# Output projections of a two-layer block on one Trainium2 core: five pairs of weight tiles as seven half-width block products

## The reference

```python
y = act @ w_out                          # 512x2048 by 2048x2048, the output projection
x = _layernorm(DEEPNORM_ALPHA * x + y, post_ln_g[i], post_ln_b[i])
x = x + (p[i] @ ple_w[i]) * jax.nn.sigmoid(x @ ple_gate_w[i])
```

## Time and profile before

| | before |
|---|---|
| median of 3 runs | 2104.14 us (2104.05 to 2104.16) |
| profiled execution, span from first to last instruction | 2101.9 us |
| what the median has around that span | 2.2 us |
| TensorE busy, of the span | 2095.9 us (100%) |
| VectorE | 1256.4 us (60%) |
| ScalarE | 818.5 us (39%) |
| GpSimd | 360.7 us (17%) |
| stretch 865 to 887 us (two tiles, layer 0): VectorE, ScalarE, GpSimd busy | 7.16, 3.83, 0 us |
| stretch 930 to 952 us (two tiles with centring): VectorE, ScalarE, GpSimd busy | 16.95, 6.75, 0 us |

### The profile page before, as it was taken

How to read it: one execution, slowest core, us unless ns; L and a number is a source line. 1 busy time by engine, 2 the same in 40 slices (tenths; PEclk the granted TensorE clock), 3 DMA queues, 4 the chain that set the end, 5 groups by cost and what they waited for, 6 DMA issues and landing times.

```text
span 2101.9 us, 28710 instructions
## 1 busy us (share of the span) xinstructions
PE 2095.9 (100%) x10510; PEld 1739.0 (83%) x10510; DVE 1256.4 (60%) x2106; ACT 818.5 (39%) x1042; POOL 360.7 (17%) x193
## 2 busy tenths in 40 slices
PE   9999999999999999999999999999999999999999
PEld 7888888888888888888788888888888888887888
DVE  5225575665755747356733588887888973567332
ACT  4224464563654657123722322222323451227221
POOL 0000000000000004000400034444757520004000
PEclk9999999999999999999999999999999999999999
DMA  8222222122122123322233322222222242222431
GB/s 318 81 100 80 81 81 80 63 77 80 62 98 80 60 80 117 136 97 100 86 124 125 135 89 92 100 100 100 94 88 99 100 179 101 88 94 79 139 112 69
DMA packets 33027, 213.62 MB, mean 102 GB/s; under 512 B 3904, under 2 KB 4176, under 8 KB 9408
## 3 DMA queue, kind: packets, MB, share of 16 engines
q1 hardware_dynamic: 28224, 189.54, 25.6%
q0 software_dynamic: 4448, 22.72, 2.8%
...
## 4 chain that ended last, share of the span: by engine, by line
PE 99%; ACT 1%; DVE 0%; issue 0%
PE G L493 91%; PE X L493 5%; PE T L493 1%; PE T L675 1%; PE T L796 0%; ACT a_hi L907 0%; ACT Z L1099 0%; ACT Y L1171 0%; PE T L801 0%; PE T L647 0%; ACT L991 0%; DVE tmp L1444 0%; PE T L671 0%; DVE Y L1446 0%; DVE tmp L1439 0%
## 5 line engine op out<-in xcount | busy, mean ns | idle before, releaser
L493 PE MATMUL G<-a_hi,w_hi 128*128 128x512 f32 (+1 forms) x2780 | 1084.5, 390 | 0.6 <-ACT a_hi L907 0.6
L493 PE MATMUL G<-a_lo,w_hi 128*128 128x512 f32 (+1 forms) x2780 | 1076.8, 388 | 0.0
L493 PE MATMUL G<-a_hi,w_lo 128*128 128x512 f32 x2764 | 1072.9, 388 | 0.0
L903 ACT ACTIVATE w_hi<-w_raw 128x2048 fp32r<-128x2048 f32 x174 | 333.4, 1916 | 957.5 <-PE G L493 944.1
L1299 DVE TENSOR_TENSOR w_lo<-w_raw,w_hi 128x2048 fp32r<-128x2048 f32 x128 | 297.1, 2321 | 643.0 <-ACT w_hi L903 643.0
L493 PEld LDWEIGHTS G<-a_hi,w_hi 128*128 128x128 f32 x2780 | 521.9, 188 | 110.5 <-ACT a_hi L907 1.5
L493 PEld LDWEIGHTS G<-a_lo,w_hi 128*128 128x128 f32 x2780 | 522.0, 188 | 107.3 <-issue 0.5
L493 PEld LDWEIGHTS G<-a_hi,w_lo 128*128 128x128 f32 x2764 | 518.9, 188 | 107.0 <-issue 0.2
L1888 DVE SCALAR_TENSOR_TENSOR T<-tmp,par,T 128x512 f32<-128x512 f32 x464 | 306.9, 748 | 0.0
L437 POOL TENSOR_TENSOR w_lo<-w_raw,w_hi 128x2048 fp32r<-128x2048 f32 x45 | 207.9, 4620 | 232.2 <-ACT w_hi L903 232.2
L405 POOL TENSOR_TENSOR a_lo<-Y,a_hi 128x512 fp32r<-128x512 f32 x32 | 44.3, 1402 | 366.7 <-ACT a_hi L907 366.4
...
## 6 DMA issues: line engine op xcount, KB each, us to landing
w_raw<-wall_in SPq DMA_DIRECT2D x174, 1024.0 KB, 4.8
...
Y<-xT_in POOLq DMA_DIRECT2D x4, 1024.0 KB, 8.2
...
Y<-x_residual POOLq DMA_DIRECT2D x4, 1024.0 KB, 5.2
...
Z<-xT_in SPq DMA_DIRECT2D x6, 512.0 KB, 9.4
```

Of the source, the lines that this page charges most:

```text
L493: return pe.matmul(o, l, r, start=start, stop=stop)
L903: f(w_hi[:, w.slot, :], w_raw[:, w.slot, :], ACT.Copy).then_inc(S("w_hi"), 1)
```

## The change

The first four tiles of the output projection are done as before (two as a pair, two by `gemm`). Tiles 4 to 13 become five pairs (`p` = 2 to 6). In each pair the first 4 of the 16 input chunks are done plainly for both tiles (pieces `r1`, `r2`: 12 matmuls of 512 columns each). The other 12 chunks are seen as two groups of 6, the two tiles as two columns and the tokens as two halves of 256; of this 2x2 by 2x2 block product seven products are formed in place of eight, each 6 blocks x 3 matmuls of 256 columns. Four of them use weights as loaded (`b11`, `b22`, `b21`, and the plain token halves) or sums of them (`t1`, `t3`, `t2`, `t4`, made by GpSimd); three kinds of combined activations are made once per layer (`fold_operands` on GpSimd, copied by ScalarE, split by VectorE: `folds`). VectorE combines the products as it takes them from PSUM (`empty_first`, `empty_products`, `finish_two`, `finish_one`). Tiles 14 and 15 are loaded and split in the same pieces but multiplied plainly (`pair_in_pieces`). Weights are split piece by piece (512 or 768 columns) into a ring of four places; GpSimd now makes the low part of `r1`, `r2` and `b22`, VectorE that of the other six. The centring moves from two chunks per tile to four chunks per pair and stands between the pieces in VectorE's row. `p_raw0` (the side input of layer 0) moves into `Y`, is loaded after the folds, and `residual(0, 3)` and all weight pieces of GpSimd wait for its split. Semaphores are merged and renamed elsewhere without another order. The host's data is unchanged.

```diff
--- before.py
+++ after.py
+PLAIN_K = 4
+PAIR_K = 6
+HALF_T = T // 2
+QUAD = PAIR_K * P
+FOLD_FROM, FOLD_TO = 2, 7
+FOLDED = ("r1", "r2", "b11", "t1", "t3", "t2", "b22", "t4", "b21")
+UNFOLDED = ("r1", "r2", "b11", "b12", "b21", "b22")
+SUMS = ("t1", "t3", "t2", "t4")
+LOW_BY_POOL = {True: ("r1", "r2", "b22"), False: ("r1", "r2", "b12")}
+RING_AT = (3328, 2560, 0, 768)
+CHAIN_AT = 1536
+PIECE_AT = {"r1": (1, 0), "r2": (0, 0), "b11": (1, PLAIN_K * P), "b21": (1, PLAIN_K * P + QUAD),
+            "b12": (0, PLAIN_K * P), "b22": (0, PLAIN_K * P + QUAD)}
...
+        def ring_free(layer, p, name):
+            n = piece_number(p, name)
+            if n < 2:
+                return S("gemm_done"), W_OUT[layer] + 2 * FOLD_FROM - 1
+            if n < 4:
+                return S("gemm_done"), W_OUT[layer] + 2 * FOLD_FROM
+            return S("piece_done"), layer * (N_PIECES - 1) + n - 3
...
+            def fold_operands(layer):
+                for i in range(PAIR_K):
+                    first, second = PLAIN_K + i, PLAIN_K + PAIR_K + i
+                    if layer == 0:
+                        pool.wait_ge(S("y_hgrn"), HEADS)
+                    else:
+                        pool.wait_ge(S("gated"), second + 1)
+                    n = layer * PAIR_K + i
+                    if i >= 2:
+                        pool.wait_ge(S("fold_lo"), n - 1)
+                    raw = fold_raw[i % 2]
+                    pool.tensor_tensor(raw[:, 0:2, :], Y4[:, first, :, :], Y4[:, first:second + 1:PAIR_K, 1, :],
+                                       ALU.subtract).then_inc(S("fold_step"), 1)
+                    pool.wait_ge(S("fold_step"), 2 * n + 1)
+                    pool.tensor_tensor(raw[:, 2, :], raw[:, 1, :], Y4[:, first, 0, :], ALU.subtract).then_inc(S("fold_step"), 1)
+                    pool.wait_ge(S("fold_step"), 2 * n + 2)
+                    pool.tensor_tensor(raw[:, 3, :], raw[:, 2, :], Y4[:, second, 0, :], ALU.add).then_inc(S("fold_raw"), 1)
+                pool.wait_ge(S("fold_raw"), (layer + 1) * PAIR_K)
+            def piece_low(layer, p, name):
+                pool.wait_ge(*high_made(layer, p, name))
+                n, at = piece_width(name), ring_slot(p, name)
+                pool.tensor_tensor(w_ring[1][at][:, 0:n], source(name), w_ring[0][at][:, 0:n].bitcast(F), ALU.subtract).then_inc(
+                    S("piece_low_pool"), 1)
+            def sum_t1(layer, p):
+                if p == FOLD_FROM:
+                    pool.wait_ge(S("gemm_done"), W_OUT[layer] + 2 * FOLD_FROM)
+                else:
+                    pool.wait_ge(*low_made(layer, p - 1, "t4"))
+                pool.wait_ge(*piece_landed(layer, p, "b11"))
+                pool.tensor_tensor(chain, piece("b11"), piece("b12"), ALU.add).then_inc(S("fold_summed"), 1)
+            def sum_t3(layer, p):
+                if p > FOLD_FROM:
+                    pool.wait_ge(*low_made(layer, p - 1, "t3"))
+                pool.wait_ge(*piece_landed(layer, p, "b22"))
+                pool.tensor_tensor(other, piece("b12"), piece("b22"), ALU.add).then_inc(S("fold_summed"), 1)
+            def sum_t2(layer, p):
+                pool.wait_ge(*low_made(layer, p, "t1"))
+                pool.tensor_tensor(chain, chain, piece("b22"), ALU.add).then_inc(S("fold_summed"), 1)
+            def sum_t4(layer, p):
+                pool.wait_ge(*low_made(layer, p, "t2"))
+                pool.wait_ge(*piece_landed(layer, p, "b21"))
+                pool.tensor_tensor(chain, chain, piece("b21"), ALU.add).then_inc(S("fold_summed"), 1)
+            def weight_pieces(layer):
+                for p in range(FOLD_FROM, FOLD_TO):
+                    piece_low(layer, p, "r1")
+                    piece_low(layer, p, "r2")
+                    sum_t1(layer, p)
+                    sum_t3(layer, p)
+                    sum_t2(layer, p)
+                    piece_low(layer, p, "b22")
+                    sum_t4(layer, p)
+                piece_low(layer, FOLD_TO, "r1")
+                piece_low(layer, FOLD_TO, "r2")
+                piece_low(layer, FOLD_TO, "b12")
 
...
+            residual(0, 0)
+            fold_operands(0)
+            pool.wait_ge(*ops_split(OPS_OUT[0], KC))
+            pool.dma_start(p_raw0, pT[0]).then_inc(S("p_landed"), 16)
+            residual(0, 1)
+            residual(0, 2)
+            pool.wait_ge(S("p_split"), 1)
+            residual(0, 3)
+            weight_pieces(0)
...
+            def piece_products(layer, p, name, out, highs, lows, start, stop):
+                pe.wait_ge(*low_made(layer, p, name))
+                hi, lo = [part[ring_slot(p, name)] for part in w_ring]
+                n = len(highs)
+                for k in range(n):
+                    at = slice(k * P, (k + 1) * P)
+                    mm(out, hi[:, at], highs[k], start and k == 0, False)
+                    mm(out, hi[:, at], lows[k], False, False)
+                    last = mm(out, lo[:, at], highs[k], False, stop and k == n - 1)
+                return last
+            def folded_pair(layer, p):
+                g = G_OUT[layer] + 2 * p
+                one, two = out_banks(p)
+                first, second = TB[0][:, 0:HALF_T], TB[1]
+                if p == FOLD_FROM:
+                    if layer == 0:
+                        pe.wait_ge(S("ms_ready"), HEADS)
+                        pe.wait_ge(S("o_copied"), HEADS)
+                        pe.wait_ge(S("kp_ready"), HEADS)
+                else:
+                    pe.wait_ge(*drained(Idx(g - 4)))
+                    pe.wait_ge(*drained(Idx(g - 3)))
+                def tokens(chunks, half):
+                    at = slice(half * HALF_T, (half + 1) * HALF_T)
+                    return [a_hi[:, c, at] for c in chunks], [a_lo[:, c, at] for c in chunks]
+                def fold(s):
+                    return [[folds[:, k, s, n, :] for k in range(PAIR_K)] for n in range(2)]
+                whole = [a_hi[:, c, :] for c in range(PLAIN_K)], [a_lo[:, c, :] for c in range(PLAIN_K)]
+                ones_at, twos_at = range(PLAIN_K, PLAIN_K + PAIR_K), range(PLAIN_K + PAIR_K, KC)
+                done = S("piece_done")
+                piece_products(layer, p, "r1", one[:, :], *whole, True, False).then_inc(done, 1)
+                piece_products(layer, p, "r2", two[:, :], *whole, True, False).then_inc(done, 1)
+                if p > FOLD_FROM:
+                    pe.wait_ge(*emptied(layer, p - 1, 6))
+                piece_products(layer, p, "b11", first, *tokens(ones_at, 0), True, True).then_inc(done, 1)
+                if p > FOLD_FROM:
+                    pe.wait_ge(*emptied(layer, p - 1, 5))
+                else:
+                    pe.wait_ge(S("fold_lo"), (layer + 1) * PAIR_K)
+                piece_products(layer, p, "t1", second[:, HALF_T:T], *fold(1), True, True).then_inc(done, 1)
+                piece_products(layer, p, "t3", second[:, 0:HALF_T], *fold(0), True, True).then_inc(done, 1)
+                if p == KC // 4:
+                    shift(*after("half_summed", 2 * layer, KC // 2 + 2), (ones_r[:, :], sum_high[:, :]))
+                pe.wait_ge(*emptied(layer, p, 1))
+                piece_products(layer, p, "t2", first, *fold(2), True, True).then_inc(done, 1)
+                piece_products(layer, p, "b22", two[:, 0:HALF_T], *fold(3), False, True).then_inc(done, 1)
+                piece_products(layer, p, "t4", one[:, HALF_T:T], *tokens(twos_at, 1), False, False).then_inc(done, 1)
+                piece_products(layer, p, "b21", one[:, 0:HALF_T], *tokens(twos_at, 0), False, True).then_inc(done, 1)
...
+                split(Idx(w + 2))
+                if layer == 0:
+                    act.wait_ge(S("o_done"), HEADS)
+                    act.wait_ge(S("ms_done"), HEADS)
+                else:
+                    act.wait_ge(S("gated"), KC)
+                fold_high(0)
+                fold_high(1)
+                split(Idx(w + 3))
+                for i in range(2, PAIR_K):
+                    fold_high(i)
                 if layer == 0:
                     act.wait_ge(S("p_landed"), 16)
...
+                half_sum(0)
+                split(Idx(w + 3))
+                half_sum(1)
+                for i in range(PAIR_K):
+                    fold_low(i)
+                if layer == 0:
+                    p_low(p_raw0, 1)
+                half_sum(2)
+                residual_in(1)
+                p = FOLD_FROM
+                piece_low(p, "b11")
+                half_sum(3)
+                piece_low(p, "t1")
+                piece_low(p, "t3")
+                piece_low(p, "t2")
+                empty_first(p)
+                piece_low(p, "t4")
+                piece_low(p, "b21")
+                empty_products(p)
+                finish_two(p)
+                half_add(5, 4)
...
+                for p in range(FOLD_FROM + 3, FOLD_TO):
+                    c = 4 * p - 17
+                    piece_low(p, "b11")
+                    finish_one(p - 1)
```

(20 more changed lines are left out.)

487 lines of the change are left out of this document (357 added, 130 removed).

## The result

The changed kernel takes 2160.77 us (2159.99 to 2161.76, 4 runs) against 2104.11 (2104.05 to 2104.16, 4 runs): ratio 1.0271, 95% interval 1.0258 to 1.0283. It is slower by 56.7 us. The forecast was 2144 us, with a range of 2110 to 2175.

A forecast was written before the change was run, and what follows sets the result against it. The prediction took TensorE's matmul stream to bound the kernel, with weights waiting for it. Its terms, -12.0 + 11 + 6 + 34 + 1 = +40 us, gave a median of 2144 us, range 2110 to 2175 for 8 in 10.

The forecast's parts named there:

- A: TensorE's matmul stream: with narrow steps of 0.120 us a pair falls from 21.76 to 20.56 us; -12.0 us.
- B: Start of layer 0: TensorE waits for `r1`'s low part behind the folds and `p_raw0`'s split; +11 us.
- C: Start of layer 1: folds delay VectorE's split of the second tile and `r1`; +6 us, ends 0.3 and 9.7.
- D: Pairs 4 to 6: GpSimd's and VectorE's work exceeds 20.56 us of matmuls, worst at `t4`; 17 us a layer, 34 together.
- E: End of the projection: the first side tile's weight copy waits for `b21`; 0.5 us a layer, +1 us.
- the high end of C: Start of layer 1: 3.7 us stall ahead of the folds plus 6 us more from collisions on each fold; 9.7 us.
- the port: SBUF access: VectorE operations with two SBUF inputs and GpSimd operations don't overlap, so their times add.
- the exclusion: GpSimd operations and VectorE's with two SBUF inputs lock each other out for the whole instruction; 4.03 us for 0.67.
- The queues hold: Rival: GpSimd and VectorE don't exclude each other, so D and E are nothing; -6 us, 2098 us; 8%.
- Each low part behind everything: Rival: all 11.6 us of GpSimd stand in VectorE's way and `p_raw0` is slow; +71 us, 2175; 15%.
- the low ends: Rival: all collisions of GpSimd and VectorE fall where they cost least; +12 us, 2116; 15%.
- bound by their weight load: Rival: the 126 narrow matmuls step near 0.19 us in place of 0.120; +76 us, over 2200; 2%.

The follow-up runs named there:

- x_fold: `x_start` with VectorE's low parts of the first two folds ahead of its split of tile 3, in both layers: 2147.74 us (1.0207).
- x_memset: The changed kernel with each GpSimd weight operation of pairs 2 to 7 replaced by two zero fills that read nothing: 2116.89 us (1.0065).
- x_psum: The changed kernel, same order, with VectorE reading the shift from PSUM and the sum of squares kept in PSUM: 2149.28 us (1.0213).
- x_order: The changed kernel with starts as in `x_fold`, VectorE's low parts earlier and centring moved to pairs 5 to 7, same operands: 2145.69 us (1.0200).
- x_start: The changed kernel with layer 0's last residual load and the split of side input p moved behind the start of pair 2: 2155.72 us (1.0248).

## Why the prediction was right, and where it was not

*Direction and range: right*, and the main cause is the one given. The size is 17 us short in the middle, by errors of both signs. The sum against its parts, in us of the profiled execution (the starts and the end are delays against the kernel before, from start to start):

| term | forecast | measured |
|---|---|---|
| A, TensorE's stream | -12.0 | -12 (narrow step 0.119) |
| B, start of layer 0 | 11 | 9.9 (one wait of 9.26) |
| C, start of layer 1 | 6 | 4.0 |
| D, the pairs, waits | 34 | 35 |
| E, the end | 1 | 8.8 |
| the clock in the pairs | none | 14 |
| ahead of the stage | none | -1.2 |
| sum | 40 | 58.5 (the spans: 58.2) |

*A: right.* All 18 narrow matmuls of a block keep the step of the earlier trace rows.

*B and C: right in mechanism, 3 us too high together.* The waits are 9.26 and 3.76 us, each ended by a GpSimd `w_lo`, in layer 0 behind `p`'s split. The path was the one described: folds without much collision (3.75 us each against 3.1 reckoned, 4.25 at the high end), `p` landed at 869. No wait came ahead of the folds in layer 1, which the high end of C had counted. Nothing in either needs the port: `x_fold` takes both away by order.

*D: right in size, and the exclusion is its main cause.* The excess of the ten pairs is 49.1 us, or 48.6 without the shift's matmul. Behind each of the six waits of 3.9 to 4.5 us 12 to 15 narrow matmuls have a step of 0.213 in place of 0.120, and the first a little more, so 1.4 to 1.5 each, 8.7; in both pairs 2 the low clock costs 2.5 (12 wide steps 0.20 longer; 23.12 in `x_memset`, where nothing else stretches that pair). That is 14 us of clock and 35 of waiting, where I had 34. By the forecast a layer's 17.8 us were 4.5 in pair 4, 7.7 in pair 5 and 5.6 in pair 6; without the clock layer 0 has about 0.9 in pair 3, 1.5 in pair 4, 8.7 in pair 5 and 5.6 in pair 6. So the split is near, and partly lucky in its total: the three centrings counted in pair 4 ran at the start of pair 5 (946.01 to 950.02), where they made a wait before `b11` (4.14) that was not named. The other long waits are before `t4` in pairs 5 and 6, as forecast.

That the waits need the exclusion is shown: with nothing read by GpSimd (`x_memset`) the pairs take 20.6 to 21.9 us, but for pair 2 of layer 0 with its low clock, and with PSUM operands single operations keep their own time. The order is the other condition: `x_psum` gave 11.5 where I expected 20 to 34, and `x_order` took the long waits out of pair 5 on the same operands, at the price of the end. How the 35 us divide between the two, no run says.

*The clock: the term that was missing.* "The sum has nothing for it", said the prediction, as no row before shows a stall. Now rows do: after 9.26 us idle the granted clock is 0.50 and twelve wide matmuls take 2.4 us more, and after 3.76 us idle, in layer 1, twelve take as much; after waits of about 4 us fourteen narrow ones take 1.3 more. The Trainium skill, "TensorE: Matmul & The Clock Gate" (Part 1), had the rule, and the trace agrees, with 0.427 in place of 0.227 a step. The prediction gave it a sentence but no number in the sum. Of the eight long waits of the profile, at 1.4 to 2.5 us each, it had forecast six, and these were there to be counted.

*E: the step that failed.* The prediction had "0.5 us a layer, between 0 and 1.5". From the last `r1` to the first side tile it is 23.39 and 22.78 us in place of 21.76, which is 2.7 together. From there to the first gate tile it is 30.73 and 29.10 in place of 26.85, another 6.1. Two waits are in that stretch in each layer: 0.92 for the bank of tile 15, which VectorE frees only behind the split, the centring and the squares of 14, and 0.67 for the last sum of squares. The term looked at the weight's copy alone and not at the queue behind it on VectorE: the rest of a layer's end is late by as much as centring is left over. In layer 0 the clock falls here too: the granted clock is 0.61 from 1033 to 1037 us, and the same two matmuls take 1.91 us there and 1.02 in layer 1, where the clock stays at 1.00. From the second sum of the layer norm on this costs 1.6 us.

```profile
1030.53 1.05 PE L739 MATMUL T<-ones_r,tmp 128*128 128x1 f32 x8 [0.68 <-DVE tmp L2053]
...
1033.09 1.91 PE L739 MATMUL X<-tmp,ones_r 128*128 128x512 f32 x2
...
1960.50 1.02 PE L739 MATMUL X<-tmp,ones_r 128*128 128x512 f32 x2
```

*Ahead of the stage*: TensorE is 1.15 us ahead of the kernel before when it reaches 828 us, 0.56 of it from the first 6 us of the program. The change has no other order of work there, and no run took this apart.

*The rivals.* "The queues hold" is out: pair 5 takes 32.4 us. "Each low part behind everything" (71) was too high, the low ends (12) too low. The narrow matmuls are not bound by their weight load: their step is 0.119.

*Left open*: why a row of GpSimd kept VectorE out for 6.95 us at 872.11, while in `x_start` the same sum beside the same row took 1.04. In the first case GpSimd was busy issuing the residual's DMA (871.89 to 872.42) when VectorE began; no run took that apart.
